# Output projections in three rounded passes, norm squares added on VectorE, the modulation's shift on ScalarE

## What is computed

```python
mod = jax.nn.silu(c) @ mod_w[l] + mod_b[l]
sh1, sc1, gt1, sh2, sc2, gt2 = jnp.split(mod, 6, axis=-1)
h = rmsnorm(x, norm1_g[l]) * (1.0 + sc1) + sh1
...
yA = rmsnorm(hseq * jax.nn.gelu(ga), rg_out_g[l])
...
o = rmsnorm(o, hg_norm_g[l]) * jax.nn.silu(gb)
y = jnp.concatenate([yA, yB], axis=-1) @ w_out[l]
x = x + gt1 * y
h2 = rmsnorm(x, norm2_g[l]) * (1.0 + sc2) + sh2
fo = swiglu(h2, ...) if l % 2 == 0 else moe_swiglu(h2, ...)
x = x + gt2 * fo
```

## Time and profile before

| | us |
|---|---|
| median of three timed runs | 1510.03 (1505.68 to 1514.51) |
| the profiled execution | 1502.89 |
| its span, first to last instruction | 1501.2 |
| TensorE busy | 1465.3 (98%) |
| VectorE busy | 1080.6 (72%) |
| ScalarE busy | 815.5 (54%) |
| mean granted TensorE clock | 0.983 |

### The profile page before, as it was taken

One profiled execution on the slowest core, in us unless ns is written; L12 is line 12 of the kernel. 1 busy time (PEld: TensorE's weight loads), 2 busy tenths in 40 slices (PEclk: granted clock), 3 DMA queues, 4 the chain that ended last, 5 costly groups with the idle time before them and its releaser, 6 DMA issues.

```text
span 1501.2 us, 22297 instructions
## 1 busy us (share of the span) xinstructions
PE 1465.3 (98%) x8559; PEld 1247.2 (83%) x8559; DVE 1080.6 (72%) x1449; ACT 815.5 (54%) x828; POOL 8.7 (1%) x29
## 2 busy tenths in 40 slices
PE   8999999999999998999999999999999999999997
PEld 4788878999988887887888888888888888888886
DVE  2588424545445764279988988899899888988995
ACT  3243433444323425246667677676676766766764
POOL 1000000000000000000000000000000000000000
PEclk9999999999999999999999999999999999999997
DMA  9986684955569723549799799798997997997960
GB/s 299 309 279 197 217 282 157 285 170 175 171 211 329 229 93 107 173 154 344 251 364 394 268 375 389 249 396 297 342 394 271 368 387 250 394 361 281 393 250 30
DMA packets 259017, 408.39 MB, mean 272 GB/s; under 512 B 9880, under 2 KB 151904, under 8 KB 258944
## 3 DMA queue, kind: packets, MB, share of 16 engines
q1 hardware_dynamic: 243712, 397.22, 75.6%
q10 hardware_dynamic: 15232, 10.18, 2.2%
HBM read 401.49 MB, written 5.95 MB: 271 GB/s over the span
## 4 chain that ended last, share of the span: by engine, by line
PE 88%; DVE 8%; ACT 3%; issue 1%; ACTq 0%; DVEq 0%
PE ps L777 20%; PE ps L778 20%; PE ps L779 19%; PE ps L660 8%; PE ps L761 4%; PE ps L868 3%; DVE slab_lo L1721 2%; PE ps L569 2%; PE ps L629 2%; PE ps L923 1%; PE ps L605 1%; DVE uT L1470 1%; PE ps L525 1%; PE ps L735 1%; PE ps L727 1%
## 5 line engine op out<-in xcount | busy, mean ns | idle before, releaser
L1721 DVE TENSOR_TENSOR slab_lo<-ring,slab_hi 128x2048 fp32r<-128x2048 f32 x264 | 603.3, 2289 | 78.8 <-ACT slab_hi L1302 78.4
L1302 ACT CAST slab_hi<-ring 128x2048 fp32r<-128x2048 f32 x261 | 497.8, 1908 | 148.8 <-PE ps L779 148.8
L777 PE MATMUL ps<-slab_hi,tokens_hi 128*128 128x512 f32 (+1 forms) x768 | 290.8, 379 | 1.9 <-DVE slab_lo L1721 1.4
L778 PE MATMUL ps<-slab_lo,tokens_hi 128*128 128x512 f32 (+1 forms) x768 | 286.9, 374 | 0.0
L779 PE MATMUL ps<-slab_hi,tokens_lo 128*128 128x512 f32 (+1 forms) x768 | 286.4, 373 | 0.0
L660 PE MATMUL ps<-hT,ring 128*128 128x264 f32 x768 | 178.1, 391 | 2.8 <-DVE hT L1449 2.8
L777 PEld LDWEIGHTS ps<-slab_hi,tokens_hi 128*128 128x128 f32 x768 | 144.3, 188 | 32.0 <-DVE slab_lo L1721 6.6
L660 PEld LDWEIGHTS ps<-hT,ring 128*128 128x128 f32 x768 | 146.2, 193 | 28.0 <-issue 3.7
L779 PEld LDWEIGHTS ps<-slab_hi,tokens_lo 128*128 128x128 f32 x768 | 144.3, 188 | 26.7
L778 PEld LDWEIGHTS ps<-slab_lo,tokens_hi 128*128 128x128 f32 x768 | 144.4, 188 | 23.5
L1669 DVE TENSOR_TENSOR slab_lo<-ring,slab_hi 128x2048 fp32r<-128x2048 f32 (+1 forms) x34 | 75.8, 2229 | 108.4 <-ACT slab_hi L1240 108.4
(11 more groups left out here) (355 smaller groups left out, 1959.4 us busy)
## 6 DMA issues: line engine op xcount, KB each, us to landing
ring<-in_moe_w SPq DMA_DIRECT2D x264, 1024.0 KB, 7.3
ring<-in_mod_w SPq DMA_DIRECT2D x48, 1024.0 KB, 8.5
ring<-in_ffn_w SPq DMA_DIRECT2D x30, 1024.0 KB, 5.6
ring<-in_w_in SPq DMA_DIRECT2D x24, 1024.0 KB, 9.9
ring<-in_w_out SPq DMA_DIRECT2D x8, 1024.0 KB, 5.9
out_new_S_sample<-S ACTq DMA_DIRECT2D x8, 512.0 KB, 2.9
ring<-in_ffn_w SPq DMA_DIRECT2D x4, 768.0 KB, 4.8
uT<-in_x_prompt SPq DMA_DIRECT2D x1, 1024.0 KB
```

The costliest lines, as they stand in the source:

```text
L777: mm(out, x, w, start=start, stop=False)
L778: mm(out, x, wl, start=False, stop=False)
L1302: cp(wH[t % 3][:, :], w).then_inc(s_hi, 1)
L1721: tt(wL[t % 3][:, :], w, wH[t % 3][:, :].bitcast(fp32), ALU.subtract).then_inc(s_lo, 1)
```

## The change

- The norms' squares are added up on VectorE (`sum_squares`, six additions a norm); TensorE does two products, one of the sum of seven squares and one of the last. The very last norm, before the outputs, stays as it was (`last_mean_square`).
- `w_out` is multiplied in three passes. ScalarE makes the high parts of `yT` and of the four slabs, VectorE the low parts. Two buffers, each with a high and a low half, hold the slabs: slabs 0 and 2 share one, 1 and 3 the other. The products of the recurrence's half of `yT` with chunks 0 to 3 come first, then the turn of the group of modulation rows, then the rest.
- The shift is added on ScalarE (`add_shift`); for the dense input ScalarE writes the high part straight from the scaled value and VectorE the low part (`low_part`).
- Groups of modulation rows: in layer 1 the first is copied ahead of the shift and the second behind it; the turn of the group ahead of the dense part moves behind the first dense slab. Their rows have another home in SBUF, and the dense slabs' two buffers change places.
- POOL's clearing of three tiles waits for the last `w_out` slab of layer 1.

```diff
-            def mean_square(n, chunks):
+            def mean_square(n):
+                pe.wait_ge(s_sum, (KC - 2) * (n + 1))
+                mm(ps[NORM_BANK[n]][:, 0:N], mean[D][:], squares[n][:, KC - 2, :], start=True, stop=False)
+                pe.wait_ge(s_sq, KC * (n + 1))
+                mm(ps[NORM_BANK[n]][:, 0:N], mean[D][:], squares[n][:, KC - 1, :], start=False, stop=True)\
+                    .then_inc(s_ms, 1)
...
-                pe.wait_ge(s_y, l + 1)
-                for g in range(4):
-                    w = slab()[:, 0:2048].rearrange("p (k n) -> p k n", k=KC)
...
+                pe.wait_ge(s_ors, l + 1)
+                w = [slab() for _ in range(4)]
...
+                for c in range(4):
+                    pe.wait_ge(s_yoL, 2 * l + 1)
+                    pe.wait_ge(s_woL, 4 * l + c // 2 + 1)
+                    out_products(c, 0, AC)
+                for g in AT_ROOTS[l]:
+                    turn_four(g)
+                for c in range(KC):
+                    if c < 4:
+                        pe.wait_ge(s_yoL, 2 * l + 2)
+                    else:
+                        pe.wait_ge(s_x1, KC * l + c - 3)
+                        pe.wait_ge(s_woL, 4 * l + c // 2 + 1)
+                    out_products(c, AC if c < 4 else 0, KC).then_inc(used if c % 2 else s_wp, 1)
+                mean_square(2 * l + 1)
...
+            def add_shift(l, which):
+                for c in range(KC):
+                    act_.wait_ge(s_hm, KC * (2 * l + which) + c + 1)
+                    A(hT[:, c, 0:T], hT[:, c, 0:T], ACT.Identity, bias=modT[:, l, 3 * which * KC + c, 0:1])\
+                        .then_inc(s_h, 1)
...
+                def out_slab(g):
+                    s_, loads, _ = SLOT["w_out", l, g]
+                    act_.wait_ge(full[s_], 16 * loads)
+                    if g >= 2:
+                        act_.wait_ge(used, USED["w_out", l, g - 2])
+                    A((woA, woB)[g % 2][:, 0, :], ring[:, s_, 0:SLAB], ACT.Copy).then_inc(s_woH, 1)
...
+            def sum_squares(n, c):
+                dve.wait_ge(s_sq, KC * n + c + 1)
+                if c > 1:
+                    dve.wait_ge(s_sum, (KC - 2) * n + c - 1)
+                tt(squares[n][:, c, :], squares[n][:, c - 1, :], squares[n][:, c, :], ALU.add).then_inc(s_sum, 1)
+
+            for c in range(1, KC - 1):
+                sum_squares(0, c)
...
+            def low_part(c):
+                dve.wait_ge(s_fhH, c + 2)
+                stt(fhL[:, c, 0:T], hT[:, c, 0:T], modT[:, 0, 3 * KC + c, 0:1], fhH[:, c, 0:T].bitcast(fp32),
+                    ALU.add, ALU.subtract).then_inc(s_fhL, 1)
```

More of the change, by code:

```diff
@@ L130, in trunk @@
             ("ffn_act_lo", FC, short)))
+        yoH, yoL, woA, woB = (nc.alloc_sbuf_tensor_at(name, shape, f32r, offset=at_) for name, shape, at_ in (
+            ("y_hi_part", [P, KC, N], h_at), ("y_lo_part", [P, KC, N], mixed),
+            ("w_out_even", [P, 2, SLAB], u_at), ("w_out_odd", [P, 2, SLAB], short + 4 * KC * N)))
+        assert 4 * KC * N <= 4 * (5 * H * P) and KC * N + 2 * SLAB <= 7 * H * N - 512
         ps = [ctx.enter_context(nc.psum_tensor(f"ps{i}", [P, 512], fp32)) for i in range(8)]
@@ L642, in gates, with products @@
                        start=True, stop=True).then_inc(s_gp, 1)
+            def products(out, x, xl, w, wl, start, stop):
+                mm(out, x, w, start=start, stop=False)
+                mm(out, x, wl, start=False, stop=False)
+                return mm(out, xl, w, start=False, stop=stop)
             def layer(l):
@@ L771, in layer @@
                         project_four(g)
[L772 to L777, removed]
-                mm(out, x, wl, start=False, stop=False)
-                return mm(out, xl, w, start=False, stop=stop)
             def dense():
@@ L816, in dense @@
                     last.then_inc(used, 1)
[L817 to L819 removed]
+                    if d == 0:
+                        for g in BEFORE_FFN:
+                            turn_four(g)
+                mean_square(2)
             def keep_busy(bank, count):
@@ L1440, in modulate @@
                 ch(tt(hs, hs, modA[:, :, 1:COND], ALU.mult))
-                ch(tt(hs, hs, shf[:, :, 1:COND], ALU.add))
-                for c in range(KC + 1):
-                    if c < KC:
-                        stt(hT[:, c, 0:T], xT[:, c, 0:T], modA[:, c, 0:1], rs[:, 0:T], ALU.mult, ALU.mult)\
-                            .then_inc(c_dve, 1)
-                        ch.n += 1
-                    if c:
-                        dve.wait_ge(c_dve, ch.n - (c < KC))
-                        ts(hT[:, c - 1, 0:T], hT[:, c - 1, 0:T], shf[:, c - 1, 0:1], None, ALU.add)\
-                            .then_inc(s_h, 1)
+                tt(hs, hs, shf[:, :, 1:COND], ALU.add).then_inc(s_hs, 1)
+                dve.wait_ge(s_hs, 2 * l + which + 1)
+                for c in range(KC):
+                    stt(hT[:, c, 0:T], xT[:, c, 0:T], modA[:, c, 0:1], rs[:, 0:T], ALU.mult, ALU.mult)\
+                        .then_inc(s_hm, 1)
+                    if feed and c == 1:
+                        dve.wait_ge(s_fhH, 1)
+                        tt(fhL[:, :, T:N], hT[:, :, T:N], fhH[:, :, T:N].bitcast(fp32), ALU.subtract)\
+                            .then_inc(s_fhL, 1)
+                    if feed and c >= 2:
+                        low_part(c - 2)
             def residual(l, part, c, bank):
@@ L1635, in layer, with out_low, out_slab @@
                     mod_four(g)
+                def out_low(half):
+                    dve.wait_ge(s_yoH, 2 * l + half + 1)
+                    k = slice(half * AC, (half + 1) * AC)
+                    tt(yoL[:, k, :], yT[:, k, :], yoH[:, k, :].bitcast(fp32), ALU.subtract).then_inc(s_yoL, 1)
+                def out_slab(g):
+                    dve.wait_ge(s_woH, 4 * l + g + 1)
+                    w_ = (woA, woB)[g % 2]
+                    tt(w_[:, 1, :], ring[:, SLOT["w_out", l, g][0], 0:SLAB], w_[:, 0, :].bitcast(fp32), ALU.subtract)\
+                        .then_inc(s_woL, 1)
+                out_low(0)
+                out_slab(0)
                 dve.wait_ge(s_ors, l + 1)
@@ L1911 @@
 MODS_NEEDED = ((1, 6, 6), (7, 11, 11))
-SECOND_SLAB = 3
+FIRST_SPLIT = 5
 U_BANKS = (0, 1, 6)
```

127 lines of the change are left out of this document (74 added, 53 removed).

## The result

The changed kernel is slower. Its median is 1515.17 us (seven executions, 1514.75 to 1522.85) against 1505.68 for the kernel before, 1.0069 of its time with a 95% interval of 1.004 to 1.0098; a second set of six gave 1.0071 (1.0051 to 1.0091). The forecast was no change; the time lies inside its range of 1499 to 1520, but the interval excludes a ratio of 1. TensorE is busy for as long as before, 1465.1 us of a span of 1518.8 against 1465.3 of 1501.2, although it has less to do: at half clock the same work is busy for longer (eight products of the state update, L753, 1.14 us at 584 and 2.06 at 589, when the clock had fallen).

A forecast was written before the change was run, and what follows sets the result against it. TensorE, holding 88% of the chain, was taken to bound the kernel. The terms +3.0 + 3.0 - 2.0 - 1.3 - 2.7 summed to 0.0 us on 1502.89, so the forecast was the runs' median, 1510, range 1499 to 1520.

The forecast's parts named there:

- the price of the half clock: After a pause, TensorE's clock was put at 0.57 for 4 us, losing 1.7 us, in both layers' output projections.
- B: Layer 0's output projection: fourth slab load, splits and half clock delay it; +3.0 us, between +1.3 and +4.2.
- E: Layer 1's projection and routing: cheaper products outweigh slab waits and half clock; -2.7 us, between -5.0 and -1.0.
- C: First feed-forward slab: TensorE starts after the root, paced by VectorE's low parts, and finishes sooner; -2.0 us.
- Rival 2: Slower: half clock at TensorE's new waits costs more per restart, slab 2's waits included; +8.4 us, 1518; chance 0.10.
- A: First norm: additions behind VectorE's setup chain delay the next projection, with some half clock; +3.0 us, between +1.5 and +3.7.
- D: Dense norms: pairs of norm squares leave the down products, final norm waits for its last addition; -1.3 us, -1.8 to +0.5.
- my five places: First norm, layer 0's projection, first feed-forward slab, dense norms, layer 1's projection with routing; together 0.0 us.

The follow-up runs named there:

- the two fillings: Six unread products before the first norm: kernel before with changed start, 1.0008; changed kernel, also one in steps 2 to 5 of both state updates, 1.0036.
- the start alone: Kernel before with only layer 0's first norm changed: six additions on VectorE behind its setup chain, two mean products on TensorE; 1.0061.
- The rest of the change alone: Changed kernel with fp32 output projections and layer 0's first norm back on TensorE; 0.9979 of the kernel before.
- the sums early: Changed kernel with the first norm's six sums ahead of VectorE's setup chain, 1.0053; with projections also in the slabs' order, 0.9911.
- the guarded: Changed kernel with six unread products before the first norm and one in each of steps 2 to 5 of both state updates; 1.0036, median 1510.45.
- the slab order: Changed kernel, each w_out slab awaited at first use, chunks 0 and 1 whole before 2 and 3: 0.9953; with first norm on TensorE, 0.9925.

## Why the prediction was wrong, step by step

**The step that failed** is the price of the half clock: "4 x 0.43 = 1.7 lost" behind a pause, counted at two places (B and E), with 1.0 in the first norm and 0.3 in C, 4.7 in all, and nothing elsewhere. It cost some 10. What the clock does can be read inside one kernel. Over the single executions of a kernel the time falls by about 1 us for each 0.001 of mean clock: 0.8 to 1.3 by straight lines through each of four sets of 21 to 29 executions of the kernel before, both sets of the changed one and those of most others (the four kernels with few executions or clocks that hardly differ give 0.5 to 1.7). The two kernels differ by 0.0103; that alone is 8 to 13 us, about the whole loss. At the same clock they are alike: the changed kernel's executions at 0.971 took 1514.8 to 1515.2, and the six of the kernel before at 0.970 to 0.972 took 1514.5 to 1517.3. One slope through 100 executions of the one and 13 of the other leaves 1.2 us between them (-0.4 to 2.8).

These lines show that time and clock go together; that the clock is the cause, and not a sign, is shown by the two fillings that add work and save time, of the start alone (1.0061 to 1.0008) and of the changed kernel (1.0071 to 1.0036). So work and waits come out even. That is not quite the forecast's sum either: its 0.0 held 4.7 of half clock, so it had put work and waits at -4.7. Rival 2 had the right mechanism, but at the new waits only, and I gave it 0.10.

The Trainium skill (TensorE: Matmul & The Clock Gate, HAM oscillation), which the forecast cited, says that a stream broken by waits pays at each restart. At the start the runs agree (0.50 for 20 us behind a pause of 5.5; with the pause filled 1.00 for the first ten of them). They add that the larger bill can come elsewhere: the state update fell from 586 behind a wait of 0.6 that the kernel before has as well.

**A, first norm, +3.0.** The mechanism was right: sums at 30.5 behind the setup chain, TensorE idle for 5.5, first w_in product 3.9 later than in the earlier trace rows. The term was not: 9 us alone, about 1 of them lateness, for which I had put 2.0, and about 8 the clock, for which I had put 1.0. In the two profiled executions of the changed kernel itself the start fell for less, and the mixer's root stood 3.4 and 3.8 later than before.

**B, layer 0's projection, +3.0.** The stage is 6.5 longer in the profiled execution, and 3.7 to 4.2 in three others with the same code there (75.0 to 75.5), inside the range. Two pieces were small. The fourth load was issued 5.1 later than in the earlier trace rows, of which 3.4 came from the stages ahead, and took 13.0 to land, not 12.0:

```profile
199.46 2.11 SPq L386 DMA_DIRECT2D ring<-in_w_out  x1
...
ring<-in_w_out SPq DMA_DIRECT2D x1, 1024.0 KB, 13.0
```

And a modulation projection ahead of it took 6.33 instead of 5.15, at half clock.

**C and D, first slab and dense norms, -3.3.** Right, at -3.1: 206.4 to 203.3, and within 1 us of that in every trace with these edits. The rest of the change alone gave 0.9979, 3 us.

**E, layer 1's projection, -2.7.** The waits came as worked out (3.9 for 4.4, 1.6 for 1.5), and without the long stretch the stage does gain: the 67.5 with the sums early is 1.8 below the 69.3 of before, and the guarded 68.6 less 1.75 of added work 2.4 below. In the profiled execution the half clock from 586 turned this into +5.3.

**What the forecast left out.** Both stretches outside my five places grew, by 3.3 and 2.2; the changed trace has half clock at 446 to 450, 542 to 546 and 658 to 672. The 3.3 is not the edits' work: the slab order with the norm on TensorE has the same edits there, no half clock, and takes 124.5 as before. No run separates the 2.2. And both projections together were called even, at +0.3, without asking for a better order; as issued they cost 7 to 9 us (with and without the changed start), in slab order they gain 8 (0.9979 to 0.9925).

**Still open:** what tips a state update into half clock in one execution and not in the next of the same kernel. None of the three traces with idle products in it shows the long stretch. Whether the new pauses, far ahead of it, make it likelier is not shown: the rest of the change alone, with neither the start's pause nor those of the three passes, has the stretch too, from 572 to 597.

```profile
571.00:581.00 10.00, 10.00 (x54) 9.92 (x54) 5.26 (x20) 4.08 (x15) 0.00 (x0) 0.59 0.35 107
```

The version that beats both is the slab order, with the first norm on TensorE or with its sums early: 0.9925 and 0.9911. The waits of the first of them in layer 0 are 1.8 for the root and none for a load or slab 2:

```profile
PE ps L670 <- ACT ar L1237: 1.8, 1, 1.8
PE ps L616 <- DVE ar L1478: 1.2, 1, 1.2
PE ps L670 <- DVE h_lo L1500: 0.5, 1, 0.5
```

## What to carry to other kernels

Work taken off TensorE is time only if TensorE still has something to do in its place: a wait put in front of light work can cost more than its own length again by the clock (at the start here about 8 us for a pause of 5.5). A stage of short products can fall to half clock without a new wait of its own, at 7 to 8 us here, so price each such stage as if it could; that a pause ahead of it is the reason was not shown. When products get cheaper than the splits that feed them, finish one operand buffer before touching the next; that was worth 17 us here.

## What the runs showed of the hardware that was not expected

- A stage whose TensorE is busy for 10.00 of 10 us can run at either clock: 91 instructions at 1.00, 58 at 0.63 with the same wait. Half clock that began inside the state update lasted for 24 to 25 us in nine profiles, until the projection was near; at the start it lasted for 21 to 29 us in seven.
- Executions of one kernel differ by 1% with their clock: the kernel before took 1502.5 at 0.983 and 1517.3 at 0.971.
- Work that nothing reads can save time: six products in a pause took 8 us off the kernel with the changed start alone. Four in each state update of the fastest version left its ratio and narrowed the spread, 16 us over twelve executions, to 6 over six. But products that outlast the wait they fill delay the work behind them, by 1.5 at layer 0's projection.
